# Attention rounds of a two-layer trunk: the transposes of the preceding pair issued ahead of the product with the values of the pair three back

## What is computed

```
def gqa_attention(q, k, v):
    ...
    def block(qi):
        s = jnp.einsum('bqkgd,bskd->bkgqs', qi, k).astype(jnp.float32) * scale
        p = jax.nn.softmax(s, axis=-1).astype(v.dtype)
        return jnp.einsum('bkgqs,bskd->bqkgd', p, v)

def mla_attention(q_nope, q_rope, k_nope, k_rope, v):
    ...
    def block(args):
        qn_i, qr_i = args
        s = (jnp.einsum('bqhd,bshd->bhqs', qn_i, k_nope)
             + jnp.einsum('bqhr,bsr->bhqs', qr_i, k_rope)).astype(jnp.float32) * scale
        p = jax.nn.softmax(s, axis=-1).astype(v.dtype)
        return jnp.einsum('bhqs,bshd->bqhd', p, v)
```

## Time and profile before

| | |
|---|---|
| time before, median of 3 runs (lowest, highest) | 1596.57 us (1595.98, 1597.22) |
| the profiled execution: its time, its span | 1597.8 us, 1595.8 us |
| mean granted PE clock in it | 0.962 of full speed |
| PE busy, DVE busy, ACT busy | 1463.9, 558.5, 438.6 us |
| attention of layer 0, of layer 1 | about 127 to 304 us, about 901 to 1079 us |

### The profile page before, as it was taken

How to read it: one execution, slowest core, us unless ns; L and a number is a source line. 1 busy time by engine, 2 the same in 40 slices (tenths; PEclk the granted TensorE clock), 3 DMA queues, 4 the chain that set the end, 5 groups by cost and what they waited for, 6 DMA issues and landing times.

```text
span 1595.8 us, 19431 instructions
## 1 busy us (share of the span) xinstructions
PE 1463.9 (92%) x7500; PEld 804.6 (50%) x7501; DVE 558.5 (35%) x1286; ACT 438.6 (27%) x1020; POOL 87.7 (5%) x96
## 2 busy tenths in 40 slices
PE   5999999999998699999779899999999948999992
PEld 1665555777745333444236555667775522334440
DVE  0056554465732311111134464454442240111114
ACT  2326565200112111121041565541100311111211
POOL 1000002000000101100000000100000000111000
PEclk9999999999999799999979999999999969999996
DMA  9526070215261799999852523401305139999984
GB/s 361 223 88 218 17 257 8 67 53 158 66 237 40 307 420 420 421 420 425 337 232 107 161 107 121 143 1 40 106 0 211 40 137 419 423 419 422 422 372 178
DMA packets 95062, 343.35 MB, mean 215 GB/s; under 512 B 13796, under 2 KB 37956, under 8 KB 80632
## 3 DMA queue, kind: packets, MB, share of 16 engines
q1 hardware_dynamic: 69152, 305.68, 48.9%
q0 software_dynamic: 9168, 28.00, 4.7%
q10 hardware_dynamic: 16648, 8.40, 1.8%
HBM read 327.34 MB, written 17.86 MB: 216 GB/s over the span
## 4 chain that ended last, share of the span: by engine, by line
PE 86%; DMA 5%; DVE 4%; ACT 2%; issue 1%; DVEq 1%; SPq 0%; POOLq 0%; ACTq 0%
PE bank L1882 18%; PE bank L1640 12%; PE bank L1590 10%; PE bank L1893 10%; PE bank L1682 7%; PE bank L1795 7%; PE bank L1697 5%; PE bank L1707 4%; PE bank L1717 4%; DMA ring<-in_w 2%; PE bank L1623 2%; PE bank L1542 2%; PE bank L1561 2%; PE bank L1848 1%; DMA ring<-in_w_ada 1%
## 5 line engine op out<-in xcount | busy, mean ns | idle before, releaser
L1882 PE MATMUL bank<-ring,reg_b 128*32 128x512 f32 (+2 forms) x1376 | 282.4, 603 | 2.9 <-ACT reg_b L1022 2.9
L1590 PE MATMUL bank<-ring,hT 128*128 128x512 f32 (+3 forms) x512 | 161.9, 478 | 3.3 <-ACT hT L870 3.3
L1882 PEld LDWEIGHTS bank<-ring,reg_b 128*32 128x32 f32 (+2 forms) x1376 | 93.8, 128 | 139.8 <-issue 135.7
L1590 PEld LDWEIGHTS bank<-ring,hT 128*128 128x128 f32 x512 | 98.7, 194 | 61.8 <-issue 35.0
L1022 ACT ACTIVATE reg_b<-bank,cur 128x128 f32<-128x128 f32 x176 | 64.0, 469 | 183.2 <-PE bank L1848 183.2
L1682 PE MATMUL bank<-reg_a,ring 128*128 128x512 f32 x256 | 112.6, 593 | 0.9 <-issue 0.9
L1893 PE MATMUL bank<-ring,reg_b 128*32 128x512 f32 (+2 forms) x544 | 113.2, 594 | 0.0
L1795 PE MATMUL bank<-ring,reg_b 128*128 128x512 f32 x256 | 112.2, 593 | 0.0
L949 ACT ACTIVATE reg_f<-bank,nmax 128x512 f32<-128x512 f32 x128 | 87.1, 684 | 61.2 <-DVE nmax L1226 60.1
L1226 DVE TENSOR_REDUCE nmax<-bank 128x1 f32<-128x512 f32 x128 | 83.8, 686 | 50.9 <-PE bank L1697 50.7
L1640 PE MATMUL bank<-hT,ring 128*128 128x256 f32 x384 | 88.1, 379 | 0.0
(11 more groups left out here) (258 smaller groups left out, 1779.8 us busy)
## 6 DMA issues: line engine op xcount, KB each, us to landing
ring<-in_w SPq DMA_DIRECT2D x74, 2048.0 KB, 24.9
ring<-in_w_ada SPq DMA_DIRECT2D x19, 2048.0 KB, 8.7
reg_a<-in_w SPq DMA_DIRECT2D x12, 2048.0 KB, 21.3
ring<-in_w_in SPq DMA_DIRECT2D x10, 2048.0 KB, 15.3
hT<-in_w SPq DMA_DIRECT2D x10, 2048.0 KB
vb<-in_w_ada ACTq DMA_DIRECT2D x16, 512.0 KB, 4.0
ring<-in_w_o SPq DMA_DIRECT2D x4, 2048.0 KB, 10.4
ring<-in_w_proj_a SPq DMA_DIRECT2D x8, 512.0 KB, 10.6
```

Source lines behind the costliest of these rows:

```text
L1590: ins = pe.matmul(bank[2 + k % 4][:, 0:n], hT[:, c, t * P:(t + 1) * P], w[:, c, :], start=c == 0, stop=c == NC - 1)
L1882: ins = pe.matmul(bank[bk][at:at + n, :], xsT[:, p % 2, c, at:at + n], slot(MOE_SLOT[j, m], NC, F)[:, c, :], start=c == 0, stop=c == NC - 1)
```

## The change

In `attend` of PE the block that issues the transposes of pair k-1 is moved up, ahead of the block with the product with the values of pair k-3. It still follows the scores of pair k and `mod_part`. Its waits move with it. No instruction is added or removed, and the orders of DVE, ACT, POOL and SP stay as they are.

```diff
                         if k < n and u0 == 0 and k % 2 == 1:
                             mod_part(k // 2)
+                        if 1 <= k < n + 1:
+                            u = u0 + k - 1
+                            for h in range(2):
+                                pe.wait_ge(pn_s, (l * UNITS + u) * 2 + (h + 1))
+                                if u >= 1:
+                                    pe.wait_ge(pt_e, (l * UNITS + u - 1) * 2 + (h + 1))
+                                for kc in range(NT):
+                                    ins = pe.transpose(bank[2 + h][:, kc * P:(kc + 1) * P],
+                                                       prob[:, u % 2, h, kc * P:(kc + 1) * P], ident)
+                                ins.then_inc(pt_r, 1)
                         if k >= 3:
                             u = u0 + k - 3
                             pe.wait_ge(pt_e, (l * UNITS + u) * 2 + 2)
                             ...
                             ins.then_inc(o_r, 1)
-                        if 1 <= k < n + 1:
-                            u = u0 + k - 1
-                            ...
-                                ins.then_inc(pt_r, 1)
```

## The result

| | |
|---|---|
| time after, median of 6 runs (lowest, highest) | 1604.76 us (1603.19, 1606.42) |
| time before beside it, median of 6 runs | 1597.85 us (1595.98, 1599.51) |
| ratio after to before, 95% interval | 1.0045 [1.0033, 1.0057] |
| profiled execution after: time, span, mean granted clock | 1604.52 us, 1602.5 us, 0.958 |
| PE, DVE, ACT busy | 1471.9, 554.2, 436.7 us |

The change costs 7.2 us by the ratio (6.9 by the two medians) where +4.2 was forecast. I call scores S, the tail pieces (`heads_product`, L1623) P and the modulation product M.

What follows compares the result with a forecast made beforehand. PE was taken as the bound, with no idle time inside the attention rounds. Stops of 2.5 us in GQA plus 1.7 in MLA gave +4.2, from 1596.57 to a median of 1600.8 us; range 1597.2 to 1604.8.

Steps and rivals of the forecast that it cites:

- (a): Attention rounds: DVE's scaling waits behind the delayed result copy, so PE's transposes wait for the scaling; +4.2 us, chance 0.62.
- `weight_sum`: MLA with u0 = 24, rounds with that step between copy and scaling: stops of 0.16, 0.35, 0.33 us, 1.7 in all.
- Its size in GQA: Even rounds 4 to 14 of the first attention: second head's transposes stop 0.21 us, twelve times, 2.5 us in all.
- The upper bound: Sum of all stops if a whole weight load of 0.105 us follows each stop: 5.2 us.
- J: Follow-up theory, not in the forecast: each junction of PE groups has a price, by whether the first weight load is hidden.
- (b): Attention rounds: transposes wait for ACT's copy, which waits for the later product with the values; hidden by cover, cost zero.
- Rounds 0 to 2 ... with it the start-up of each call: Start of each attention call: no product with the values there, so order and start-up waits stay unchanged; cost zero.
- All instructions stay, so PE's work is the same sum: Whole kernel: reordering leaves PE's work unchanged, so the only effect is new waits in rounds 3 to n.
- The cover holds: Rival: DVE is quick enough in GQA, only `weight_sum` rounds stop; +0.5 to +1.7 us, all under +3.2 counted, chance 0.26.
- The clock falls: Rival: PE's clock drops after stops in the twelve short GQA rounds, 12 us, 1613; chance 0.10 shared with later chains.
- stops of 0.61 and 0.44 us: Evidence against the clock rival: stops at the start of MLA that left the clock at 1.00.
- PE idle in attention should grow by 4 us: Sign expected in the trace after: PE's idle time grows by 4 us in attention and nowhere else.

Runs made afterwards that it cites:

- the own bank alone: Kernel before the change, with the product with the values of each call's last pair in bank 7 instead of bank 1; ratio to before 0.9980 [0.9967, 0.9992].

## Why the prediction was right and where it failed

*Direction and mechanism of (a): right.* The new wait is T's wait for DVE's second scaling, in even rounds of GQA and in the rounds with a `weight_sum`, and the delayed copy on DVE is its cause: moving the copy takes the waits away, doubling it lengthens them by the whole copy. The second head was ready at v + 2.75 to the hundredth.

*Its size in GQA: right but for a term that was put too low.* Forecast 0.21 a round, measured 0.25 (the pair of rounds takes 8.28 us for 8.03): 12 x 0.25 = 3.0 for 2.5. The term is the weight load after a stop, 0.05 from the earlier trace rows. The half T behind the stop takes 0.59 for 0.51, so 0.08. The upper bound, a load of 0.105, was nearer.

*`weight_sum`: right.* Forecast 0.16, 0.35 and 0.33. The rounds take 3.94, 4.13 and 4.13 for 3.77, +0.17, +0.36 and +0.36: 1.8 us for 1.7, of which some 0.04 each is J.

*(b), the rounds: right.* ACT starts its copies at v + 1.20 (149.67), for 1.14 forecast, and no T of a full round waits for it.

*"Rounds 0 to 2 ... with it the start-up of each call": failed.* The order of rounds 0 to 2 stays, but a start-up's wait can reach into round 3, and there the old order had V in front of T as cover. In the kernel after T of pair 2 in u0 = 24 starts only when ACT has emptied the bank:

```profile
274.13 0.91 PEld L1707 LDWEIGHTS bank<-cst,reg_f 128*128 128x128 f32 x8 [1.08 <-DVE reg_f L1220]
274.16 1.12 PE L1707 MATMUL bank<-cst,reg_f 128*128 128x128 f32 x8 [0.28 <-ACT reg_c L957]
```

That round takes 4.14 us, 0.37 more than the 3.77 before. In layer 1 slower scores covered it. The call with u0 = 16 has a smaller one, 0.09. That ACT is the releaser is read from the row; no run separates it.

*"All instructions stay, so PE's work is the same sum": failed. This is the step that failed, and the largest miss, 1.9 of the 3.0 us by which the sum fell short: it put the price of the new neighbours on PE at nothing.* The sum of the work is the same, its price in the chain is not. J costs 6 x 0.23 = 1.4 us in the tails, which the prediction took as untouched, and 0.04 to 0.05 in each round of MLA without a stop, some 0.5 us with what there is at the start of u0 = 16. The forecast even read the difference without seeing it: the earlier trace rows show 1.94 and 1.72 for groups that stand behind a T, and the new order puts them behind a V.

By terms: 3.0 (GQA) + 1.8 (`weight_sum`) + 1.4 (tails) + 0.5 (rounds of u0 = 16) + 0.1 (round 4 of u0 = 24, two layers) + 0.4 (start-up) = 7.2 us. Forecast were 2.5 + 1.7 + 0 + 0 + 0 + 0. The range's upper end was 1604.8 for the median, +8.2, since it had a clock fall and a half in it, and the real 7.2 came from something else: the profiled executions of before and after have one fall each, in layer 1. That the median lies just within that end is luck. The stops alone were given 3.3 to 5.2 us, and 7.2 is above that.

*The rivals.* "The cover holds" was wrong: all twelve rounds waited. "The clock falls" at the short stops was wrong too: the granted clock stayed 1.00 in the window 140 to 190 us with its six stops, at the level of 2.4 GHz. The "stops of 0.61 and 0.44 us" that the prediction brought against this rival were no stops of PE: they are idle times of the weight load (the earlier trace rows have the first), and PE's own row had none there at the first and 0.20 us at the second. "PE idle in attention should grow by 4 us" could not have been seen, as the busy time above shows.

The Trainium skill, "TensorE: Matmul & The Clock Gate", Part 2, says in "Step-by-step: what each phase is for" that PE pulls a weight load ahead of matmuls in flight if their row groups don't conflict or if it goes to the background weight buffer. The traces show such a pull where T follows S of MLA or S follows T, and none where S follows V; whether the page's conditions held there, no row tells. These are rows of the kernel after, PE and its weight loads:

```profile
229.11 1.98 PE L1697 MATMUL bank<-reg_b 96*128 96x512 f32 x4
230.93 1.04 PE L1707 MATMUL bank<-cst,reg_f 128*128 128x128 f32 x8
...
229.11 0.30 PEld L1697 LDWEIGHTS bank<-reg_b 96*128 96x128 f32 x2 [0.17 <-ACT reg_f L949]
...
230.51 0.14 PEld L1707 LDWEIGHTS bank<-cst,reg_f 128*128 128x128 f32 x1 [0.24 <-issue]
```

And of the kernel before, where S follows T:

```profile
229.88 1.88 PE L1697 MATMUL bank<-reg_b 96*128 96x512 f32 x4
...
229.78 0.30 PEld L1697 LDWEIGHTS bank<-reg_b 96*128 96x128 f32 x2
```

T's first load starts 0.42 us ahead of its first matmul behind S. That of S starts 0.10 ahead behind a T, and together with the matmul's row, not ahead of it, behind a V. The row of S behind V names ACT's exponential (L949), which ends just before it, so a wait for ACT would be a rival to J. It falls by the kernel with the result copied twice: there the exponential of the same round ends later, at 232.27, than S's load starts, and S still takes 1.91 us in the chain.

```profile
231.95 0.30 PEld L1699 LDWEIGHTS bank<-reg_b 96*128 96x128 f32 x2 [0.17 <-issue]
```

Why V shuts it out (its weights are 64 columns wide, and its two heads take turns) no run here tells.

## What to carry to other kernels

Before a group is moved on an engine that is the bound, price each new pair of neighbours, not only the groups: look up in the trace what each group takes behind each predecessor, and count tails and the first full round as well. Then follow what the group that was pushed back releases (here a copy that stood at the head of another engine's queue) and measure the distance to the group pulled forward. And where the bound engine waits in a tail for a buffer, as 0.44 us for one bank here, a free buffer is worth more (0.2%) than any order of the rounds that was tried.

## What was not expected of the hardware

- The first weight load of a group costs up to 0.19 us in the chain (1.91 against 1.72 for the same four matmuls, 2.13 against 1.94 for the same six), by what stands ahead of it.
- The scaling on DVE takes 2.12 us in place of 0.49 where POOL's sums over 128x1024 elements run. Timeline of the kernel after, u0 = 24:

```profile
265.46 2.54 POOL L782 TENSOR_TENSOR ring<-hT,ring 128x1024 f32<-128x1024 f32 x1 [0.18 <-POOL hT L780]
...
266.17 2.12 DVE L1220 TENSOR_SCALAR reg_f<-reg_f,linv 128x512 f32<-128x512 f32 x1
```

  It ends at 268.29, 0.29 us after POOL's instruction. The next scaling, which began 1.8 us into POOL's next sum (268.18 to 270.53), took 0.84 us and ended 0.28 after it. The Trainium skill, "SBUF — State Buffer", "Terms", says that DVE and POOL have a port pair in common that one holds for a whole instruction while the other is blocked; the rows agree with that.
- That scaling stops PE for 1.8 us, and what follows is not the same each time. In the profiled executions of before and after the next four scores took 1.88 us in layer 0 and 2.91 and 3.14 in layer 1 (rows of PE). The granted clock of the kernel after was 1.00 from 268 to 272 us and 0.57 from 1045 to 1049 us, so a good part of the latter went by at 1.2 GHz. Of the 24 such stops in the twelve kernels, with one profiled execution each, 13 had such slow scores, a fall, behind them: 8 of 10 where DVE's copy is moved, 5 of 14 elsewhere, none with the own bank alone. Whether the moved copy makes it more likely, so few can't tell. One fall costs about 1.1 us of attention (177.46 and 178.56 in the two layers of one kernel), or 0.6 where a start-up wait goes with it (u0 = 24 of the kernel after: 60.42 and 61.03). A fall more or less in each layer is 2.2 us, two thirds of what the own bank gains: a reason to compare segments, not only totals.
